# The last two hidden chunks of both FFNs tile by tile, a weight block loaded in eight pieces, and the softmax scale on ScalarE, in a two-block model kernel

## What is computed

```python
def rms_norm(x, g):
    return x * lax.rsqrt(jnp.mean(x * x, axis=-1, keepdims=True) + EPS) * g

def swiglu(hn, w_gate, w_up, w_down):
    return (jax.nn.silu(hn @ w_gate) * (hn @ w_up)) @ w_down

def rwkv7_time_mix(h, mu, w_r, w_k, w_v, w_o, ...):
    xx = jnp.pad(h, ((0, 0), (1, 0), (0, 0)))[:, :-1] - h
    xr, xw, xk, xv, xa, xg = [h + xx * mu[i] for i in range(6)]
    ...
    k = xk @ w_k
    ...
    y = wkv7_scan(rh, decay, kh, vh, -kk, kk * ah)
    ...
    return (y * g) @ w_o, v_first
```

## Time and profile before

| | |
|---|---|
| median of three runs | 1094.57 us (1094.16 to 1095.48) |
| the profiled execution | 1095.36 us |
| its span | 1093.5 us |
| TensorE busy | 1068.1 us, 98% |
| VectorE busy | 797.6 us, 73% |
| ScalarE busy | 544.5 us, 50% |
| granted TensorE clock | full in every slice |
| chain that ended last | TensorE 83%, VectorE 11%, ScalarE 2%, DMA 2%, issue 2% |

### The profile page before, as it was taken

The page is one execution under the profiler, slowest core; times in us unless marked ns, Lnnn a source line. Parts: engine busy times, 40 slices in busy tenths (PEclk is TensorE's granted clock), DMA queues, the critical chain, the costliest instruction groups (busy, mean ns, idle before and its releaser), DMA issues.

```text
span 1093.5 us, 18176 instructions
## 1 busy us (share of the span) xinstructions
PE 1068.1 (98%) x7390; PEld 900.9 (82%) x7390; DVE 797.6 (73%) x1063; ACT 544.5 (50%) x679; POOL 52.1 (5%) x65
## 2 busy tenths in 40 slices
PE   9999999999999998999999999999999999999997
PEld 8887888888778777788888888888967888999996
DVE  5665668677699789766767768999997877555554
ACT  6545533436465535363443556474645665444443
POOL 0000000001200450000000011000000000000000
PEclk9999999999999999999999999999999999999999
DMA  9697888766444221479888685475521553555632
GB/s 315 230 275 244 282 299 274 264 246 193 120 154 135 75 51 43 154 265 338 277 274 288 197 263 155 146 231 164 193 79 53 189 183 116 188 197 167 216 118 113
DMA packets 140844, 212.16 MB, mean 194 GB/s; under 512 B 20968, under 2 KB 97069, under 8 KB 140526
## 3 DMA queue, kind: packets, MB, share of 16 engines
q1 hardware_dynamic: 135908, 203.11, 55.8%
q0 software_dynamic: 2080, 7.37, 2.7%
q10 hardware_dynamic: 2794, 0.80, 0.4%
HBM read 205.49 MB, written 7.87 MB: 195 GB/s over the span
## 4 chain that ended last, share of the span: by engine, by line
PE 83%; DVE 11%; ACT 2%; DMA 2%; issue 2%; POOL 0%; ACTq 0%; DVEq 0%
PE ps L812 24%; PE ps L814 24%; PE ps L813 24%; DVE wl L2608 2%; PE ps L1038 2%; PE ps L1286 2%; PE ps L1705 1%; PE ps L889 1%; DMA raw<-in_rwkv_w_k 1%; PE ps L1223 1%; PE ps L1687 1%; ACT wh L1828 1%; DMA wide<-vectors 0%; PE ps L866 0%; DVE wide L3553 0%
## 5 line engine op out<-in xcount | busy, mean ns | idle before, releaser
L2608 DVE TENSOR_TENSOR wl<-raw,wh 128x2048 fp32r<-128x2048 f32 (+2 forms) x154 | 344.6, 2248 | 97.0 <-ACT wh L1828 96.8
L812 PE MATMUL ps<-wh,xh 128*128 128x512 f32 (+3 forms) x856 | 334.9, 391 | 3.8 <-DVE xl L2678 1.8
L814 PE MATMUL ps<-wl,xh 128*128 128x512 f32 (+3 forms) x856 | 328.2, 383 | 0.0
L813 PE MATMUL ps<-wh,xl 128*128 128x512 f32 (+3 forms) x856 | 327.9, 383 | 0.0
L1828 ACT ACTIVATE wh<-raw 128x2048 fp32r<-128x2048 f32 (+2 forms) x154 | 286.5, 1878 | 32.4 <-PE ps L814 27.2
L812 PEld LDWEIGHTS ps<-wh,xh 128*128 128x128 f32 x856 | 160.8, 188 | 37.7 <-DVE xl L2678 2.7
L814 PEld LDWEIGHTS ps<-wl,xh 128*128 128x128 f32 x856 | 160.8, 188 | 31.7
L813 PEld LDWEIGHTS ps<-wh,xl 128*128 128x128 f32 x856 | 161.0, 188 | 30.1 <-issue 0.7
L812 PE MATMUL ps<-wh,gh 128*128 128x512 f32 x288 | 112.6, 391 | 0.0
L813 PE MATMUL ps<-wh,gl 128*128 128x512 f32 x288 | 112.2, 390 | 0.0
L814 PE MATMUL ps<-wl,gh 128*128 128x512 f32 x288 | 112.1, 389 | 0.0
(11 more groups left out here) (455 smaller groups left out, 1271.7 us busy)
## 6 DMA issues: line engine op xcount, KB each, us to landing
wide<-in_w_ada SPq DMA_DIRECT2D x48, 512.0 KB, 5.3
raw<-in_ffn_w_gate SPq DMA_DIRECT2D x44, 512.0 KB, 4.2
raw<-in_ffn_w_up SPq DMA_DIRECT2D x44, 512.0 KB, 5.3
raw<-in_ffn_w_down SPq DMA_DIRECT2D x22, 1024.0 KB, 5.0
raw<-in_w_mlp_in SPq DMA_DIRECT2D x16, 1024.0 KB, 7.2
raw<-in_w_mlp_out SPq DMA_DIRECT2D x16, 1024.0 KB, 5.0
raw<-in_w_in SPq DMA_DIRECT2D x16, 512.0 KB, 5.3
raw<-in_w_in SPq DMA_DIRECT2D x8, 1024.0 KB, 5.2
```

The lines of the kernel that those rows point to most:

```text
L812: pe.matmul(o, lh, rh, start=start, stop=False)
L813: pe.matmul(o, ll, rh, start=False, stop=False)
L814: return pe.matmul(o, lh, rl, start=False, stop=stop)
L2608: v.tensor_tensor(wl[:, s, 0:width], raw[:, s, 0:width], f32(wh[:, s, 0:width]), ALU.subtract).then_inc(lo_ready[s], 1)
```

## The change

**FFN tails.** The loops of both FFNs end one chunk sooner. On TensorE `tail()` does the second half of the last gate and up, the down products of the last two chunks and the last turned product by tile, all of tile 0 first; the next norm's first transposes stand before the last three products. The other engines' work has the same order.

```diff
+                def tail():
+
+                    i = NFFN - 2
+                    pe.wait_ge(S(f + ".h"), B(f + ".h") + i + 1)
+                    gu_half(0, i + 1, 4)
+                    hidden_transposes(f)
+                    pe.wait_ge(lo_ready[1], uses[1] + i + 2)
+                    quarter(1, range(4, 8), 0, ps[:, 4, :], False, True).then_inc(S(f + ".out"), 1)
+                    pe.wait_ge(S(f + ".gl"), B(f + ".gl") + i + 1)
+                    pe.wait_ge(lo_ready[2], uses[2] + i + 1)
+                    down_tile(0, 0)
+                    turn_last(0)
+                    down_tile(1, 0)
+                    quarter(1, range(4, 8), 1, ps[:, 5, :], False, True).then_inc(w_used[1], 1)
...
+                    for n in range(2):
+                        last_down_part(0, n, 0)
+                        last_down_part(0, n, 1).then_inc(S(f + ".out"), 1)
+                    turn_last(1)
+                    down_tile(0, 1)
+                    down_tile(1, 1).then_inc(w_used[2], 1)
...
+                    last_down_part(1, 0, 0)
+                    last_down_part(1, 0, 1).then_inc(S(f + ".out"), 1)
+                    last_down_part(1, 1, 0)
+                    tile_transposes(turned_first, 0)
+                    last_down_part(1, 1, 1).then_inc(w_used[0], 1)
```

`down_tile(j, t)` and `last_down_part(t, n, j)` are 6 and 3 matmuls, `turn_last(t)` is two transposes. Behind it, on TensorE, the rank products go by tile and fillers are left out, and in `first_glu` the transposes of tile 1 stand behind the second quarter:

```diff
             hT, xx = W3(0, KT), W3(1, KT)
-            spin(7, 4)
-            tile_transposes("mix1", 0)
-            spin(7, 8)
-            tile_transposes("mix1", 1)
             pe.wait_ge(S("rw_w1"), B("rw_w1") + 48)
-            for part, x in enumerate((hT, xx)):
-                for t in range(NT):
+            for t in range(NT):
+                if t == 1:
+                    tile_transposes("mix1", 1)
+                for part, x in enumerate((hT, xx)):
...
                 o = [ps[:, t, :] for t in range(NT)]
-                spin(7, 12)
-                tile_transposes("pre", 0)
                 s0, s1 = arrive(("glu", 0, 0)), plan.at["glu", 0, 1][0]
                 spin(7, 8)
                 pe.wait_ge(S("pre.xl"), B("pre.xl") + 2)
-                quarter(s0, range(0, 4), 0, o[0], True, False)
-                tile_transposes("pre", 1)
+                quarter(s0, range(0, 4), 0, o[0], True, False, spare[0])
                 arrive(("glu", 0, 1))
                 pe.wait_ge(S("pre.xl"), B("pre.xl") + 4)
                 quarter(s1, range(4, 8), 0, o[0], False, True)
+                tile_transposes("pre", 1)
                 pe.wait_ge(S("pre.xl"), B("pre.xl") + 6)
```

**The o block.** Eight DMAs of 128x256 in place of four of 128x512, with the second of each pair paced by a count of four:

```diff
                 for a, step in enumerate(("gkv", "mt", "r1", "m2")):
-                    sp.wait_ge(S("wkv." + step), B("wkv." + step) + 3)
                     r0, n0 = O_ORDER[2][1] * 512 + a * P, O_ORDER[2][0] * 512
-                    sp.dma_start(wl_plain[:, s * SLOT + a * 512:s * SLOT + (a + 1) * 512], SRC["o"][r0:r0 + P, n0:n0 + 512])\
-                      .then_inc(raw_loaded[s], 16)
+                    for i in range(2):
+                        sp.wait_ge(S("wkv." + step), B("wkv." + step) + 3 + i)
+                        c0 = s * SLOT + a * 512 + i * 256
+                        sp.dma_start(wl_plain[:, c0:c0 + 256], SRC["o"][r0:r0 + P, n0 + i * 256:n0 + (i + 1) * 256]).then_inc(raw_loaded[s], 16)
```

**Attention.** The scale by the reciprocal of the sum goes from VectorE to ScalarE:

```diff
+            def scaled(i):
+                b = i % 2
+                act.wait_ge(S("at.r"), B("at.r") + i + 1)
+                for t in range(NT):
+                    nk = P * (t + 1)
+                    act.activation(pp[b][:, t, 0:nk], pp[b][:, t, 0:nk], ACT.Copy, scale=arec[:, 2 * b + t:2 * b + t + 1]).then_inc(S("at.p"), 1)
+
             split(("attn_out", 0, 1))
             for i in range(0, NH, 2):
                 exps(i)
                 if i:
+                    weights_T(i - 1)
                     out_hi(i - 2)
-                    weights_T(i - 1)
+                scaled(i)
                 exps(i + 1)
-                weights_T(i)
                 if i:
                     out_hi(i - 1)
+                weights_T(i)
+                scaled(i + 1)
...
-                link(v.reciprocal(arec[:, 2 * b:2 * b + 2], asum[:, 2 * b:2 * b + 2]))
-                for t in range(NT):
-                    nk = P * (t + 1)
-                    v.tensor_scalar(pp[b][:, t, 0:nk], pp[b][:, t, 0:nk], arec[:, 2 * b + t:2 * b + t + 1], None, ALU.mult)\
-                     .then_inc(S("at.p"), 1)
+                v.reciprocal(arec[:, 2 * b:2 * b + 2], asum[:, 2 * b:2 * b + 2]).then_inc(S("at.r"), 1)
```

More of the change, by code:

```diff
@@ L836, in half, with quarter @@
                 return m
-            def quarter(s, kts, t, o, start, stop):
+            def quarter(s, kts, t, o, start, stop, home=None):
+                hi, lo = home or (wh[:, s, :], wl[:, s, :])
                 for j, kt in enumerate(kts):
                     w = slice(j * 512, (j + 1) * 512)
-                    m = mm3(o, xh[:, kt, tok(t)], xl[:, kt, tok(t)], wh[:, s, w], wl[:, s, w], start and j == 0, stop and j == len(kts) - 1)
+                    m = mm3(o, xh[:, kt, tok(t)], xl[:, kt, tok(t)], hi[:, w], lo[:, w], start and j == 0, stop and j == len(kts) - 1)
                 return m
@@ L923, in body @@
+                def body(i, first):
                     if not first:
@@ L1904, in copy_hi, with ffn_loop, units @@
                        .then_inc(S(name + ".xh"), 1)
-            def ffn_loop(f, uses, loads, per, fn, before_gh=None, after_gh=None, after_first=None):
+            def ffn_loop(f, uses, loads, per, fn, after_first=None, between=None, after_last_unit=None):
                 def gu(k, c):
                     split_hi(k, uses[k] + c, loads[k] + per[k] * c + per[k])
[L1910 to L1914, removed]
+                def units(i):
+                    gu(0, i + 1)
                     act.wait_ge(w_used[1], uses[1] + i + 1)
@@ L1930, in body @@
                     act.wait_ge(S(f + ".mT"), B(f + ".mT") + 1)
-                    act.activation((xh if last else gh)[:, 0:2, :], ps[:, 6, :].rearrange("p (a n) -> p a n", a=2), ACT.Copy).then_inc(S(f + ".gh"), 1)
-                    if not last:
-                        split_hi(2, uses[2] + i, loads[2] + per[2] * i + per[2])
-                    elif after_gh:
-                        after_gh()
+                    act.activation(gh[:, 0:2, :], ps[:, 6, :].rearrange("p (a n) -> p a n", a=2), ACT.Copy).then_inc(S(f + ".gh"), 1)
@@ new lines, in ffn_loop @@
+                turned_units(i)
+                split_hi(0, uses[0] + NFFN, loads[0] + per[0] * NFFN + per[2])
+                act.wait_ge(S(f + ".h"), B(f + ".h") + i + 1)
+                act.wait_ge(S(f + ".out"), B(f + ".out") + 1)
+                last_units(0)
+                last_turned(0)
+                if between:
+                    between()
+                act.wait_ge(w_used[1], uses[1] + NFFN)
+                last_units(1)
+                after_last_unit()
+                last_turned(1)
@@ L2333, in second_glu_block, with fin_std @@
                 act.activation(wh[:, s, 1024:SLOT], raw[:, s, 1024:SLOT], ACT.Copy).then_inc(hi_ready[s], 1)
-            ffn_loop("ffn1", u_, l_, (32, 32, 16), ACT.Silu, lambda: split(("glu", 0, 0)), second_glu_block, late_vectors)
-            for t in range(NT):
+            ffn_loop("ffn1", u_, l_, (32, 32, 16), ACT.Silu, late_vectors, first_glu_block, sqrt_table)
+            def fin_std(t):
                 act.wait_ge(S("ffn1.add"), B("ffn1.add") + 2 * (t + 1))
@@ L2733, in body @@
                         v.wait_ge(S(f + ".mT"), B(f + ".mT") + i)
[L2734 to L2743 removed]
+                    unit(i, 0)
@@ L2747, in body @@
                      .then_inc(S(f + ".gl"), 1)
-                    if not last:
-                        split_lo(2, uses[2] + i)
-                for i in range(NFFN):
-                    body(i, i == NFFN - 1)
+                for i in range(NFFN - 2):
+                    units(i)
+                    turned_units(i)
+                    split_lo(2, uses[2] + i)
+                i = NFFN - 2
+                units(i)
+                split_lo(2, uses[2] + i)
+                turned_units(i)
@@ L3350, in _, with first_glu_rest, second_glu_rest @@
-            v.wait_ge(S("fin.u"), B("fin.u") + 4)
+            s_glu, use_glu, _, _ = plan.at["glu", 0, 1]
+            def first_glu_rest():
+                s, use, _, _ = plan.at["glu", 0, 0]
+                v.wait_ge(hi_ready[s], use + 1)
+                v.tensor_tensor(spare[0][1][:, :], raw[:, s, :], f32(spare[0][0][:, :]), ALU.subtract).then_inc(lo_ready[s], 1)
+            def second_glu_rest(part):
+                o = slice(1024 * part, 1024 * part + 1024)
+                if part == 0:
+                    v.wait_ge(S("glu.half"), B("glu.half") + 1)
+                else:
+                    v.wait_ge(hi_ready[s_glu], use_glu + 1)
+                m = v.tensor_tensor(wl[:, s_glu, o], raw[:, s_glu, o], f32(wh[:, s_glu, o]), ALU.subtract)
+                if part:
+                    m.then_inc(lo_ready[s_glu], 1)
```

209 lines of the change are left out of this document (132 added, 77 removed).

## The result

The changed kernel took 1097.53 us in the median of ten executions (1095.70 to 1099.16), the kernel before 1094.55 beside it: a ratio of 1.0023, 95% interval 1.0014 to 1.0032. It is **slower by 3.0 us by the medians and by 2.5 by the ratio**, whose interval is 1.5 to 3.5 us, and outside the range of 1090.9 to 1095.2. A ratio here is not exactly the quotient of the two medians; where the two differ by more than the point at issue, both are given. Two disturbed executions, 2760.45 in e1 and 1162.15 of the kernel before beside e5 to e8, are left out of the ratios, and without the first the median of e1 is 1098.41.

The account below looks back on a forecast made before the run. The prediction took TensorE, busy 1068.1 of 1093.5 us, as the bound nearly everywhere. Its terms, -0.3 + 0.2 - 1.1 - 0.3 = -1.5 us, took 1094.6-level runs to a median of 1093.1 us, range 1090.9 to 1095.2.

Parts of the forecast that it names:

- the sum: Whole kernel: four terms of -0.3, +0.2, -1.1 and -0.3 make -1.5 us, for a median of 1093.1 us.
- rival (D): Glu stretch: the granted clock falls to 1.2 GHz, 24 products take 5.4 us more, 1098.5 us in all; chance 0.08.
- The waits themselves: TensorE waits about 0.7, 1.4 and 2.1 us before k, 2.0 and 2.7 us around the first glu quarters.
- First FFN to k: From the first FFN's end to the k products: tile order brings k to 274.4, -0.3 us, bounds 0 and -2.3.
- Second FFN to glu: From the second FFN to glu: first quarter 2.5 us sooner, gain lost in one wait; +0.2 us, bounds +0.5 and -2.5.
- The o block: Wkv stage: half-size pieces and code blocks ending 24 products later shorten the 2.25 us stop; -1.1 us, bounds 0 and -2.25.
- Attention: Attention heads: 16 scalings move from VectorE to ScalarE, next scores come sooner, once; -0.3 us, bounds -0.6 and +0.5.

Follow-up runs that it names:

- e1: The changed kernel with 22 instead of 8 fillers before the first glu quarter and 20 behind the transposes of tile 1: 1098.64 us, ratio 1.0030.
- e5: The changed kernel with 15 fillers before the first glu quarter and 10 behind the transposes of tile 1: 1095.06 us, ratio 1.0007.
- e8: e7 with the first half of the first k block's low part ahead of the norm of tile 0 on VectorE: 1091.81 us.
- e3: The kernel before without its 20 fillers ahead of the first glu quarter: 1097.32 us, ratio 1.0021.
- e4: The kernel before with only the o block in eight pieces instead of four: 1094.18 us, ratio 0.9996.
- e9: e8 with the transposes of tile 1 between the two rank products of tile 0, 3 fillers ahead of them: 1091.30 us, ratio 0.9961.
- e6: e5 with fillers also in the three waits before the k products: 1095.62 us, ratio 1.0011.
- e10: The kernel before without its 12 fillers ahead of the k products: 1096.00 us, ratio 1.0003.
- e16: The kernel before once more, unchanged, for its trace: 1094.65 us in that execution.
- e2: The changed kernel with the transposes of tile 1 between the two glu quarters of tile 0: 1092.95 us, ratio 0.9979.
- e12: e6 with the o block in four pieces: 1095.83 us, ratio to e6 1.0001.
- e11: e6 with the softmax scale back on VectorE: 1095.98 us, ratio to e6 1.0010.
- e15: The changed kernel once more, unchanged, as a fourth trace: 1101.05 us in that execution.
- e7: e6 with the transposes of tile 1 between the two glu quarters of tile 0, without fillers behind them: 1091.79 us, ratio 0.9976.

## Why the prediction was wrong, point by point

- **What failed is that the sum took the fillers away at no price, and left their price to rival (D) with a chance of 0.08,** because "TensorE was idle for 2.25 us at 417.82 and kept 1.00". One wait in dense work says nothing of two waits of 2.0 and 2.6 us with 24 products and transposes between them. The waits themselves were forecast rightly. e3 shows that 20 fillers were worth 2.8 us in the kernel before, and e5 that fillers in the two glu waits take the falls out of D. The Trainium skill's sentence that activity releases the throttle ("TensorE: Matmul & The Clock Gate", "What's actually happening") agrees with e3, where the clock is 0.50 to 0.53 behind the idle time and 1.00 in the earlier trace rows with the fillers.
- **(D)'s price and place were off too.** 5.4 us for 24 slow products; measured 8 slow products and 1.6 us a fall (B 26.78 against 25.18; D 231.6 against 230.0), one to three of them, and also behind the waits before k, which was not named.
- **First FFN to k, -0.3:** A is 30.84 in all four traces of the changed kernel, against 30.73 and 31.16 in the two of the kernel before and 30.83 and 30.90 in e3 and e4, so -0.1. That k came within 0.1 us of the time laid is partly luck: A's first marker stood 0.34 sooner in this execution (243.60 against 243.94), ahead of anything that the term is about. And its reading, that the k block's split gave back what the tile order would bring, holds by half: with half of it out (e8) nothing moved. The ranks of tile 0 ahead of tile 1's transposes bind as well (e9).
- **Second FFN to glu, +0.2:** D without a fall is 228.4 (e5, e6) against 227.4 to 228.1, mean 227.7 (before, e4, e10, e16): +0.7, just over the upper bound of +0.5. D covers much more than this place, but the difference is there by the third quarter. The step was right: the second quarter ahead of tile 1's transposes gives the gain back, and e2 takes 2.7 us of it.
- **The o block, -1.1:** mis-sized. The stop of 2.25 was taken as a cost that each execution pays; it is 2.25 in two traces and 1.13 in the third by the same code (before, e3, e16), and C differs by 0.5 between them. C is 148.1 to 150.8, mean 149.2, in the twelve traces of kernels with the change and eight pieces, and 149.0 to 150.2, mean 149.5, in the five of before, e3, e4, e10 and e16. So -0.3, within the scatter; e4 and e12 see nothing. That the piece in flight delays the code's fetch is not shown by any run.
- **Attention, -0.3:** -0.62, in every trace with the scale on ScalarE. The first weights' transposes come 0.25 later and the next scores 0.25 sooner, as laid; small waits of the following heads, which I took as none, give the other 0.4.
- **The sum.** Measured terms without falls are -0.1, +0.7, -0.3 and -0.6, so -0.3; with two falls of 1.6, +2.9, and +3.0 was measured by the medians. With an interval of 1.5 to 3.5 and stretch C between 148.1 and 150.8, an agreement to 0.1 is luck.

**What stays open.** By that sum e5 and e6 should be about 0.3 us under the kernel before; their medians are 0.7 and 1.2 above those beside them. The traces of e11 and e12 give no sign that the scale or the o block is the cause. The traces of e5 and e6 (1094.65, 1094.63) lie under their medians, so what the other executions have more is not in a trace that I hold. One candidate, not shown: stretch C, which differs by 2.7 us between traces without a fall in it (148.15 in e11, 150.83 in e15), is 148.42 in e6's trace, 0.8 under the mean. Falls are not tied to the changed places alone: e12's trace has one in C, between 400 and 405, and ten of 32 executions of the kernel before have a mean clock of 0.998 or less. But a mean clock of 0.998 doesn't prove a fall that costs anything: e7's trace has 0.998 with the low level only in its last 3.5 us, behind TensorE's last product. How often which place falls is known from few traces.

## What to carry to other kernels

Before a filler or a short wait in front of a large product is moved, read the granted clock behind it in several executions, not one: price a fall by products at either level, and give it more than the chance of an accident when the change leaves waits like the 2.0 and 2.6 us here in a row. Look also where in the trace the low level stands, since behind the last product it costs nothing. When work goes by tile, look at what the last tile's chain needs first: here a transpose 2.7 us too late on TensorE gave back a whole FFN's reordering. A difference read from one trace of a stop that has no releaser is good to about 1 us.

## What the runs showed of the hardware

- A filler of two fp32 records took 0.22 us (e1: 22 in 4.83 us), so fillers that end too late can cost more than a fall that they prevent: D is 230.87 in e1 and 228.37 in e5, 2.5 us for 1.6.
- The clock can fall in the middle of products that follow a wait, not in the wait: in the changed kernel three products behind the wait of 2.62 ran at 2.4 GHz, then eight at 1.2 GHz.
- Stops of TensorE without a releaser in the wkv stage moved with the place of the code and were up to 2.3 us long; their sum between 411 and 427 was 1.6 to 3.6 us, and the length of the stage did not follow it (e4: 3.55 and 149.47; e1: 1.57 and 149.76).
